# Reordering TensorE's work at the start of each head pair of an RWKV-7 stage, and moving one transpose

## The reference, cut to what matters

```python
def step(S, inp):
    r_t, w_t, k_t, v_t, kk_t, a_t = inp
    sa = jnp.einsum('bhvk,bhk->bhv', S, -kk_t)
    S = (S * w_t[:, :, None, :] + sa[..., None] * (kk_t * a_t)[:, :, None, :]
         + v_t[..., None] * k_t[:, :, None, :])
    y = jnp.einsum('bhvk,bhk->bhv', S, r_t) if emit else None
    return S, y
```

## Time and profile before

| | before |
|---|---|
| median of 3 runs | 4046.11 us |
| the profiled execution: its own time | 4042.38 us |
| its span, first to last instruction | 4040.7 us |
| PE busy | 3837.3 us (95%) |
| DVE busy | 2498.4 us (62%) |
| ACT busy | 1731.9 us (43%) |
| share of PE in the chain that ended last | 82% |
| mean granted TensorE clock | 0.976 |
| RWKV-7 stage, from its first key norms to the last scan | about 705 to 1355 us |

### The profile page before, as it was taken

The page is one execution under the profiler, slowest core; times in us unless marked ns, Lnnn a source line. Parts: engine busy times, 40 slices in busy tenths (PEclk is TensorE's granted clock), DMA queues, the critical chain, the costliest instruction groups (busy, mean ns, idle before and its releaser), DMA issues.

```text
span 4040.7 us, 86831 instructions
## 1 busy us (share of the span) xinstructions
PE 3837.3 (95%) x36296; PEld 3259.2 (81%) x36296; DVE 2498.4 (62%) x4413; ACT 1731.9 (43%) x3152; POOL 272.9 (7%) x437
## 2 busy tenths in 40 slices
PE   6999999899889999989999999999999999899999
PEld 3788888566666899989999999878677778787879
DVE  2544587656555686777888777754553553646365
ACT  2544333334334445455444444443343442534354
POOL 0000011232222100000000000000000000000000
PEclk7999999899999999999999999999999999999999
DMA  9422566465555686556666666532223232433335
GB/s 365 150 79 66 195 230 202 150 179 179 179 170 174 203 284 231 196 186 192 224 215 219 219 214 218 176 120 85 73 69 93 63 120 96 134 114 95 117 98 188
DMA packets 289442, 662.45 MB, mean 164 GB/s; under 512 B 21088, under 2 KB 31328, under 8 KB 287536
## 3 DMA queue, kind: packets, MB, share of 16 engines
q1 hardware_dynamic: 233392, 441.74, 33.8%
q0 software_dynamic: 55680, 215.34, 16.8%
HBM read 639.17 MB, written 17.83 MB: 163 GB/s over the span
## 4 chain that ended last, share of the span: by engine, by line
PE 82%; DVE 9%; ACT 3%; issue 3%; DMA 2%; SPq 0%; POOL 0%; DVEq 0%; ACTq 0%; POOLq 0%
PE psum L861 63%; PE psum L826 2%; PE psum L1123 2%; DVE wlo L2212 1%; PE psum L1173 1%; PE psum L886 1%; ACT whi L1577 1%; PE psum L841 1%; DMA ada_head<-in_w_ada 1%; PE psum L1478 1%; DVE smx L2969 1%; PE psum L1188 1%; PE psum L1054 1%; PE psum L964 1%; PE psum L948 1%
## 5 line engine op out<-in xcount | busy, mean ns | idle before, releaser
L2212 DVE TENSOR_TENSOR wlo<-raw,whi 128x512 fp32r<-128x512 f32 (+3 forms) x1568 | 1049.3, 681 | 993.6 <-ACT whi L1577 984.5
L1577 ACT ACTIVATE whi<-raw 128x512 fp32r<-128x512 f32 (+3 forms) x1568 | 969.7, 623 | 1467.9 <-PE psum L861 1442.4
L861 PE MATMUL psum<-hhi,whi 128*128 128x512 f32 (+1 forms) x2416 | 831.3, 344 | 35.2 <-DVE hlo L2252 16.9
L861 PE MATMUL psum<-hlo,whi 128*128 128x512 f32 (+1 forms) x2416 | 811.9, 336 | 0.0
L861 PE MATMUL psum<-hhi,wlo 128*128 128x512 f32 (+1 forms) x2416 | 811.9, 336 | 0.0
L861 PEld LDWEIGHTS psum<-hhi,whi 128*128 128x128 f32 x2416 | 461.7, 191 | 129.7 <-issue 54.4
L861 PEld LDWEIGHTS psum<-hlo,whi 128*128 128x128 f32 x2416 | 462.1, 191 | 46.6 <-issue 2.2
L861 PEld LDWEIGHTS psum<-hhi,wlo 128*128 128x128 f32 x2416 | 461.4, 191 | 47.5
L861 PE MATMUL psum<-fhi,whi 128*128 128x256 f32 x1408 | 401.5, 285 | 19.8 <-DVE wlo L2212 15.3
L861 PE MATMUL psum<-flo,whi 128*128 128x256 f32 x1408 | 400.2, 284 | 0.0
L861 PE MATMUL psum<-fhi,wlo 128*128 128x256 f32 x1408 | 400.0, 284 | 0.0
(11 more groups left out here) (433 smaller groups left out, 7030.3 us busy)
## 6 DMA issues: line engine op xcount, KB each, us to landing
raw<-in_w_in SPq DMA_DIRECT2D x328, 512.0 KB, 3.8
ada_raw<-in_w_ada POOLq DMA_DIRECT2D x192, 512.0 KB, 4.5
red_raw<-in_w_adaT POOLq DMA_DIRECT2D x128, 512.0 KB, 4.5
raw<-in_w_out SPq DMA_DIRECT2D x96, 512.0 KB, 3.7
raw<-in_w_gate SPq DMA_DIRECT2D x88, 512.0 KB, 4.4
raw<-in_w_val SPq DMA_DIRECT2D x88, 512.0 KB, 4.2
raw<-in_w_down SPq DMA_DIRECT2D x88, 512.0 KB, 4.3
ada_head<-in_w_ada SPq DMA_DIRECT2D x64, 512.0 KB, 10.4
```

The source lines that it names most:

```text
L861: mm = pe.matmul(dst, l, r, start=(k == 0 and i == 0 and first), stop=(k == nch - 1 and i == 2), skip_group_check=True)
L1577: act.activation(whi[:, lc % HL, 0:width], raw[:, (lc // 2) % RAW, lc % 2, 0:width], ACT.Copy).then_inc(w_hi, 1)
L2212: dve.tensor_tensor(wlo[:, lc % HL, 0:width], raw[:, (lc // 2) % RAW, lc % 2, 0:width], whi[:, lc % HL, 0:width].bitcast(F32), ALU.subtrac ...
```

## The change

Three edits, all in the order of steps that exist already. No step is added or taken away.

- The first pair's `chunk_pairs(first_done, 0)` waits for DVE's `rs` instead of `abk0`, two labels later.
- The start of an iteration becomes `be0`, `ada(0, 0)`, `trv`, the wait for ACT, `al1`, `B01`. The start of the first iteration no longer has its own waits for `rs` and `I0`. It has the wait of the others, for all labels so far, which in iteration 0 is the whole of `FIRST_DVE`, and `I0` is its last label.
- `tb1` moves behind `w0`, `ada(1, 0)` and `X13`/`Y13` on PE, and behind `w0`, `X13` and `Y13` on ACT.

```diff
-        RW_PE = ["be0", "al1", "trv", "B01", "ta0", "B11", "X01", "Y01", "tb0", "X11", "Y11", "be1"]
+        RW_PE = ["be0", "trv", "al1", "B01", "ta0", "B11", "X01", "Y01", "tb0", "X11", "Y11", "be1"]
...
-        RW_PE += ["B03", "kn", "B13", "ta1", "X03", "Y03", "tb1", "w0", "X13", "Y13"]
+        RW_PE += ["B03", "kn", "B13", "ta1", "X03", "Y03", "w0", "X13", "Y13", "tb1"]
...
-        RW_ACT += ["ta1", "X03", "Y03", "tb1", "w0", "X13", "Y13", "P10", "w1", "a0", "nx", "X04", "Y04", "tk1", "X14", "Y14", "a1", "E0"]
+        RW_ACT += ["ta1", "X03", "Y03", "w0", "X13", "Y13", "tb1", "P10", "w1", "a0", "nx", "X04", "Y04", "tk1", "X14", "Y14", "a1", "E0"]
...
-            pe.wait_ge(rw_dve, at(FIRST_DVE, "abk0"))
+            pe.wait_ge(rw_dve, at(FIRST_DVE, "rs"))
             chunk_pairs(first_done, 0)
...
-                if it == 0:
-                    pe.wait_ge(rw_dve, at(FIRST_DVE, "rs"))
-                else:
-                    pe.wait_ge(rw_dve, it * len(RW_DVE) + len(FIRST_DVE))
+                pe.wait_ge(rw_dve, it * len(RW_DVE) + len(FIRST_DVE))
                 from_keys(0)
+                ada(0, 0)
+                pe.wait_ge(v_in, it * 16 + 16)
+                turn(v_t, "trv")
                 pe.wait_ge(rw_act, it * len(RW_ACT) + len(FIRST_ACT))
                 chunk_pairs(done, 1)
-                pe.wait_ge(v_in, it * 16 + 16)
-                turn(v_t, "trv")
-                ada(0, 0)
-                if it == 0:
-                    pe.wait_ge(rw_dve, at(FIRST_DVE, "I0"))
                 level_b(0, 1)
...
                 level_xy(0, 3)
-                act_at("ta1")
-                turn(b_s[1], "tb1")
                 lora_rows(done, "w0", lambda: pe.wait_ge(rw_in, it * 80 + 160))
                 ada(1, 0)
                 level_xy(1, 3)
+                act_at("ta1")
+                turn(b_s[1], "tb1")
                 ada(1, 1)
...
-                turned("tb1", b_tok[1])
                 lora_out(done, "w0", pe_at)
                 x_out(1, 3)
                 y_out(1, 3)
+                turned("tb1", b_tok[1])
```

## The result

The changed kernel takes 4071.5 us, the median of 4 runs (4065.65 to 4073.46), beside 4045.26 us for the kernel before in runs on the same chip. The ratio is 1.0063 with a 95% interval of 1.0047 to 1.008: slower by 26 us, or 19 to 32. The forecast was 4069.4 us, 23.3 us more. The profiled execution took 4070.89 us, with a mean granted clock of 0.974.

A forecast was written before the change was run, and what follows sets the result against it. PE was taken to bound the kernel, with `al1`, DVE's `I1` and `B11` on its path. The terms 8.1 + 7.2 + 8.0 = 23.3 us on a median of 4046.11 gave 4069.4 us, range 4059 to 4079.

The forecast's parts named there:

- `I1` behind `al1`, 7 x 1.15 us: Start of iterations 1 to 7: `al1` ends 1.15 us later, so DVE's `I1` and PE's `B11` do too; 8.1 us.
- The first iteration, 7.2 us: Iteration 0: `be0` must wait for `I0`, which needs `al0`, so `B11` starts at 742.1 instead of 734.96.
- The lower end of 4.4: First iteration's lower bound: if PE's clock rises right at 732.7, `be0` to `al1` take half and 4.4 us remain.
- `tb1`, 8 x 1.0 us: Each iteration: ACT copies `tb1` out later, behind table load and sigmoid, so `B04` starts 1.0 us later; 8.0 us in all.
- drain: At ACT's table load: the skill's rule adds about 1.38 us, making the `tb1` term 19 us; the trace showed none.
- I find no place that takes a delay of PE back.: From `B11` to the end of an iteration: engines wait for each other in turn, so no PE delay is recovered.
- the first rival: PE's stalls after `v_tok` in iterations 3 to 7 each shrink by 1.15 us: 5.8 us back, 4063.6 us; chance 0.19.
- The second rival: New idle times lower PE's clock: 13 us more if in half of 16 gaps, 4082.4 us; chance 0.13.
- The sum, 23.3 us: Whole kernel: 8.1 + 7.2 + 8.0 us slower, 0.58%; chance 0.58 as it stands.
- The other two rivals: Delays hidden by DVE's scan chain, 4049.3 us, chance 0.05; PE's clock back sooner, so faster, chance 0.05.

The follow-up runs named there:

- second profile of before: The kernel before, unchanged, run and profiled once more: 4050.85 us.
- the thin kernels: Kernels before and after, `ada` weight transfers in the stage cut to 64 of 512 columns, each read four times: 4017.48 us (0.9912 of before) and 4040.56 us (0.9966).
- the head alone: The changed kernel without the moves of `tb1`, against the kernel before: 4067.54 us, 1.0034.
- the two kernels with the loop's order: Only `be0`, `ada(0, 0)`, `trv`, `al1` reordered in the loop, first waits as before: 4059.65 us, 1.0017 of before; with 64-column transfers 4027.41 us, 0.9936.
- the last kernel above: Kernel before with `bon` ahead of the second `ada_final`, DVE's bias behind the bonus, `ada(0, 2)` ahead of `B11`: 4047.57 us, 0.9985.

## Why the prediction was right, and what was wrong in it

- **`I1` behind `al1`, 7 x 1.15 us.** Right in its mechanism. PE's idle time went from 0.34 to 1.64 us, 1.3 and not 1.15. DVE starts 0.07 us behind the end of `al1` in both kernels. The difference lies on PE, whose remaining work is through earlier: `B01` starts 0.17 us ahead of the end of `al1` (825.71 and 825.88), where `trv` started 0.07 ahead of it. From `rs` to `B11` the seven iterations together grew by 8.1 us, as summed. That they agree so well is luck in part: they grew by 0.05 to 2.3 us each, since a part of `be0` runs at the lower clock in some, and by 9.7 us in all against the second profile of before.
- **The first iteration, 7.2 us.** 7.4 in the profile. (The forecast's own terms add up to 741.96 and so to 7.0 us; 742.1 and 7.2 are rounded up on the way.) Alone, the new waits cost 5.0 us up to `B11` and 6.5 in time. The lower end of 4.4, with the clock at its upper level from 732.7 on, did not come: the matmuls of `ada(0, 0)` still took 1.01 us from start to start.
- **`tb1`, 8 x 1.0 us.** Right: 0.82 to 0.97 us idle in each of eight iterations, 8.9 us for this part alone. The table load took 1.28 us and the sigmoid started 0.01 us behind it in every iteration, so that no drain was in the way here either.
- **"I find no place that takes a delay of PE back."** This step failed. The stalls of iterations 3 to 7 shrank from 7.96 to 1.7 us, about 6 us, as the first rival priced it (5.8). Against the second profile of before, where they were 7.5 us, it is the same. The reason against it was that what starts them may lie behind `B11`. In iteration 5 the packet does start behind `B11`, by 4.4 us before and 3.1 us after. But it doesn't move with `B11`: it keeps its time behind the start of the iteration. The reason given for it, transfers of POOL that come earlier, is not shown. The share of transfers in their length is, by the thin kernels.
- **The clock.** The second rival came in part too. Three of the seven later iterations have a stretch at the lower clock right behind the new idle time. In sums by stretch (columns as in the earlier trace rows):

```profile
829.00:834.00 5.00, 4.40 (x108) 3.98 (x108) 3.31 (x5) 0.89 (x2) 1.58 (x3) 0.66 0.45 135
911.00:916.00 5.00, 4.71 (x110) 3.98 (x110) 3.00 (x5) 1.38 (x3) 1.27 (x3) 0.66 0.46 135
990.00:994.00 4.00, 3.96 (x100) 3.83 (x100) 2.69 (x4) 0.43 (x1) 1.02 (x2) 0.57 0.52 168
```

  The same stretch behind `B11` before:

```profile
817.00:822.00 5.00, 5.00 (x226) 3.87 (x223) 2.08 (x3) 3.09 (x6) 2.76 (x5) 1.00 0.81 248
```

  A mean of 0.66 over 5 us is 3.4 us at 1.2 GHz, which costs 1.7 us of PE's work; three are an estimated 5 us. In the profiles, such stretches right behind `B11` stand only in the five kernels with the 1.64 us idle: 3 in after, 3 in after with thin transfers, 1 in the head alone, 1 and 2 in the two kernels with the loop's order; none in the eight kernels without it. The Trainium skill (Perfetto Trace Analysis, Matmul Optimizations) asks for matmuls back to back in batches since the engine scales its power with its use; that spoke against this change, and by this estimate it cost about a fifth of what was lost. Over the whole stage the mean granted clock is 0.94 in both profiles of before and 0.93 after. It is 0.93 with `tb1` alone as well, which has no 1.64 us of idle time, so a single profile doesn't tell how much of the rest belongs to the change.
- **The sum, 23.3 us.** The stalls gave back 6 us and the clock took 5, and the forecast held because the two cancel. That they cancel is luck. That each of the three terms holds is not: each shows as a wait of its size in the profiles, and in the two thin kernels, without the give-back, the stage grew by 28.6 us, which is the sum and the clock's 5. In the profiles with full transfers 23.3 - 6.3 + 5 makes 22.0 us, and the stage grew by 22.6. The other 5.9 us of the span's 28.5 lie outside the stage, where the kernels don't differ. Why the measured 26.2 us are 2.9 more than the sum stays open; the interval of 19 to 32 holds both.
- **The other two rivals** did not come. The delays were not hidden: `B11` and `B04` came later in their turn, and the time rose. The clock did not come back sooner: its mean in the stage fell by 0.01.

## What to carry to other kernels

When the bounding engine waits for a chain on another engine, ask which of its steps starts the chain and which only fill the time: a step moved ahead of the starter costs its whole length, though the engine does the same work. A copy that shares a memory bank with a later product is paid behind each thing queued ahead of it, here a table load and three activations. A stall without a semaphore that doesn't move with the work ahead of it is a hidden sink: delays ahead of it are partly free, and gains ahead of it are partly lost. Find out when it ends, counted from the start of the iteration, before pricing a shift, and at which number in the engine's own stream of instructions it stands: here every such stall of PE stood where a new packet of 256 instructions began. And when two effects of 5 and 6 us that nobody summed cancel, a forecast that comes true says little about either.

## What was not expected of the hardware

- PE runs out of instructions. It stops for 0.5 to 2.1 us in iterations 3 to 7 of the two profiles of before, and goes on 1.25 to 1.51 us behind the landing of a 16 KB packet of instructions; in iteration 5 other transfers take 0.63 of the DMA engines at that place. With the weights' transfers at an eighth of their size (0.27) the stop is 0.5 us at most. The kernel before gains 36 us by that, more than the 7 to 20 expected and far more than the 8 us of these five stalls. In the whole stage such stops of over 0.25 us fall from 25.8 to 3.2 us; the rest of the gain was not taken apart.
- Idle times of 1.64 us are followed by a drop of the clock in some iterations and not in others (1 to 3 of the 7 later ones, in each kernel that has them). Of the five stalls of 1.35 to 1.76 us behind `B11` in the first profile of before none was followed by one, but a stall of 1.60 us that ends at 1029.65 in the same profile was, 0.17 us later, and so was one of 1.68 us in iteration 0 of the second profile. Of the stalls of 1.77 to 2.12 us in the last kernel above two of six were. What decides is open.
